# Masks by source tile and an earlier sum of two directions in the head stage of an mLSTM / HGRN2 block

## The reference, cut to what matters

```python
M_HEADS = 8; M_DK = 64; M_DV = 128

def mlstm_scan(q, k, v, ig, lf, state):
    causal = jnp.tril(jnp.ones((L, L), dtype=bool))
    def step(carry, xs):
        ...
        d = jnp.where(causal, b[..., :, None] - b[..., None, :] + ic[..., None, :], -jnp.inf)
        m_t = jnp.maximum(inter, jnp.max(d, axis=-1))
        s = jnp.einsum('bhtd,bhsd->bhts', qc, kc) * jnp.exp(d - m_t[..., None])
        num = jnp.einsum('bhts,bhsv->bhtv', s, vc) + ...
        den = jnp.sum(s, axis=-1) + ...
        h = num / jnp.maximum(jnp.abs(den), jnp.exp(-m_t))[..., None]
    ...

def bidirectional_scan(scan_fn, ctx_fwd, ctx_bwd, lat_fwd, lat_bwd, state0):
    hc_f, st_f = scan_fn(*ctx_fwd, state0)
    hc_b, st_b = scan_fn(*[_flip_t(a) for a in ctx_bwd], state0)
    hl_f, _ = scan_fn(*lat_fwd, st_f)
    hl_b, _ = scan_fn(*[_flip_t(a) for a in lat_bwd], st_b)
    return hc_f + _flip_t(hc_b), hl_f + _flip_t(hl_b)
```

## Time and profile before

| | us |
|---|---|
| median of 3 runs | 1911.44 (1909.27 to 1913.52) |
| the profiled execution's own time | 1908.46 |
| its span | 1906.7 |
| head stage, in the span | 206.0 to 294.7 |
| PE busy in the span | 1787.2 (94%) |
| POOL busy in the span | 132.1 (7%) |

### The profile page before, as it was taken

One profiled execution on the slowest core, in us unless ns is written; L12 is line 12 of the kernel. 1 busy time (PEld: TensorE's weight loads), 2 busy tenths in 40 slices (PEclk: granted clock), 3 DMA queues, 4 the chain that ended last, 5 costly groups with the idle time before them and its releaser, 6 DMA issues. The chain is left out here.

```text
span 1906.7 us, 23789 instructions
## 1 busy us (share of the span) xinstructions
PE 1787.2 (94%) x8836; PEld 1475.6 (77%) x8836; DVE 1372.7 (72%) x1457; ACT 1032.7 (54%) x1249; POOL 132.1 (7%) x138
## 2 busy tenths in 40 slices
PE   7999887899999998899997869999999999999997
PEld 2688676787887876788886758888888888888886
DVE  3676378755554555677449558898989898989898
ACT  2543454522122125422344447888888787878775
POOL 2251120000000000100003020000000000000002
PEclk9999898899999999899998969999999999999999
DMA  7544253444433552344220339999999999999996
GB/s 270 177 144 144 67 188 101 159 144 150 159 133 112 180 184 99 111 166 155 100 77 1 148 117 342 347 407 356 401 355 404 354 402 355 404 350 405 354 407 223
DMA packets 148809, 436.23 MB, mean 229 GB/s; under 512 B 8395, under 2 KB 31091, under 8 KB 148606
## 3 DMA queue, kind: packets, MB, share of 16 engines
q1 hardware_dynamic: 146232, 430.92, 61.5%
q0 software_dynamic: 1152, 4.19, 0.6%
q10 hardware_dynamic: 1350, 0.11, 0.1%
HBM read 416.59 MB, written 16.25 MB: 227 GB/s over the span
## 5 line engine op out<-in xcount | busy, mean ns | idle before, releaser
L2910 DVE TENSOR_TENSOR w_low<-e_ring,w_high 128x1536 fp32r<-128x1536 f32 x383 | 611.6, 1621 | 84.7 <-ACT w_high L2814 83.9
L2814 ACT ACTIVATE w_high<-e_ring 128x1536 fp32r<-128x1536 f32 (+1 forms) x381 | 520.1, 1380 | 157.9 <-PE ps L2732 126.0
L2730 PE MATMUL ps<-w_high,list_h 128*128 128x512 f32 (+1 forms) x768 | 290.6, 378 | 4.2 <-DVE list_l L2928 4.2
L2732 PE MATMUL ps<-w_high,list_l 128*128 128x512 f32 (+1 forms) x768 | 286.8, 373 | 0.0
L2731 PE MATMUL ps<-w_low,list_h 128*128 128x512 f32 (+1 forms) x768 | 286.7, 373 | 0.0
L1791 ACT ACTIVATE fw_high<-ring 128x1024 fp32r<-128x1024 f32 x62 | 65.7, 1060 | 263.2 <-PE ps L1720 191.2
L1842 DVE TENSOR_TENSOR fw_low<-ring,fw_high 128x1024 fp32r<-128x1024 f32 x62 | 76.0, 1225 | 149.8 <-ACT fw_high L1791 149.7
L2730 PEld LDWEIGHTS ps<-w_high,list_h 128*128 128x128 f32 x768 | 144.8, 188 | 25.9 <-issue 4.6
L2732 PEld LDWEIGHTS ps<-w_high,list_l 128*128 128x128 f32 x768 | 144.6, 188 | 21.2
L2731 PEld LDWEIGHTS ps<-w_low,list_h 128*128 128x128 f32 x768 | 144.9, 189 | 20.7
L1718 PE MATMUL ps<-u_high,fw_high 128*128 128x512 f32 x352 | 141.0, 400 | 7.8 <-DVE fw_low L1842 7.8
(11 more groups left out here) (450 smaller groups left out, 3349.6 us busy)
## 6 DMA issues: line engine op xcount, KB each, us to landing
e_ring<-in_e_w_gu_dram SPq DMA_DIRECT2D x96, 1536.0 KB, 9.1
e_ring<-in_e_w_down_dram SPq DMA_DIRECT2D x48, 1536.0 KB, 8.7
bg_area<-in_mod_w_dram SPq DMA_DIRECT2D x72, 512.0 KB, 4.2
e_ring<-in_e_w_gu_dram SPq DMA_DIRECT2D x32, 1024.0 KB, 7.9
ring<-in_f_w_gu_dram SPq DMA_DIRECT2D x22, 1024.0 KB, 7.8
ring<-in_h_w_in_dram SPq DMA_DIRECT2D x10, 2048.0 KB, 8.4
e_ring<-in_e_w_down_dram SPq DMA_DIRECT2D x16, 1024.0 KB, 7.1
ring<-in_m_w_in_dram SPq DMA_DIRECT2D x6, 2048.0 KB, 8.3
```

The lines of the kernel that those rows point to most:

```text
L2730: nc.tensor.matmul(out, high[:, f, :], w_high[:, c, :], start=(f == 0), stop=False)
L2732: last = nc.tensor.matmul(out, low[:, f, :], w_high[:, c, :], start=False, stop=(f == total - 1))
L2814: nc.scalar.activation(piece(k.w_high, p), raw_piece(k, p), ACT.Copy).then_inc(S.high_done, 1)
L2910: nc.vector.tensor_tensor(piece(k.w_low, p), raw_piece(k, p), piece(k.w_high, p).bitcast(F32), ALU.subtract).then_inc(S.low_done, 1)
```

## The change

POOL's mask is cut in four: one instruction for each source tile, each behind that tile's own weighing, where one instruction for all four stood behind the last weighing. PE's one wait for the mask of a turn becomes a wait for each target tile, for the mask of the last source tile it has. And POOL adds a head's two directions in the even turn that follows them, where it was in the odd one after that.

```diff
             def values(n):
                 h, d = n // 2, n % 2
-                pe.wait_ge(masked, n + 1)
                 if n >= 2:
                     pe.wait_ge(summed, n - 1)
                 for i in (0, 1, 2, 3) if d == 0 else (1, 2, 3, 0):
                     js = SOURCES[d][i]
+                    pe.wait_ge(masked, 4 * n + max(js) + 1)
                     if n and i == (3 if d == 0 else 0):
                         pe.wait_ge(summed, n)
...
             for n in range(turns):
                 d = n % 2
-                pool.wait_ge(probs, 4 * n + 4)
-
-                flat = k.u_area[:, d * NT * T:(d + 1) * NT * T]
-                diag = bass.AP(flat.tensor, flat.offset, [list(flat.ap[0]), [T + P, NT], [1, P]])
                 sign = 1 if d == 0 else -1
-                pool.affine_select(out=diag, in_=diag, compare_op=ALU.is_ge, fill=0.0, base=0,
-                                   pattern=[[0, NT], [sign, P]], channel_multiplier=-sign).then_inc(masked, 1)
-                if d == 1 and n > 1:
+                for j in range(NT):
+                    pool.wait_ge(probs, 4 * n + j + 1)
+                    diag = prob[:, d, j, j * P:(j + 1) * P]
+                    pool.affine_select(out=diag, in_=diag, compare_op=ALU.is_ge, fill=0.0, base=0,
+                                       pattern=[[sign, P]], channel_multiplier=-sign).then_inc(masked, 1)
+                if d == 0 and n:
                     add(n // 2 - 1)
             add(HEADS - 1)
```

## The result

Over 20 executions each the changed kernel took 1917.14 us (1910.89 to 1920.94), the kernel before 1909.57 (1900.30 to 1921.39); ratio 1.0037, 95% interval 1.0023 to 1.0051. The forecast was 1912.7 in a range of 1907.5 to 1916.0, most likely within 0.2%. It was wrong: the time lies 1.1 us above the range, and the change costs some 7 us instead of 1.3. The profiled execution took 1913.7 us with a span of 1911.9, so the profile shows a milder case than the median.

A forecast was written before the change was run, and what follows sets the result against it. The head stage, a chain from one head's scores to the next, was taken as the only place of gain or loss; +0.3 at head 2, becoming about 0.5, then +1.0 -0.4 +1.0 -0.4 -0.4 made +1.3: 1912.7 us, range 1907.5 to 1916.0.

The forecast's parts named there:

- Turn 0, masks by tile: Turn 0 of the head stage: value sums start sooner behind per-tile masks, leaving -0.7 us at the end of head 1's scores.
- Masks elsewhere, waits on PE: Other turns: sooner masks are off the path and worth nothing; 48 more PE waits were also taken as nothing.
- What the earlier sum frees: Heads 3 and 5: without L1334's wait for POOL each takes 8.31 us, -0.4 us each, -0.8 together.
- What it runs into: Turns 2, 4 and 8: POOL's sum meets two DVE subtractions, costing 1.03 us each, +3.1 us on the path.
- Rival A: Turns 2, 4 and 8: VectorE keeps its ports through both subtractions, so no cost; 1908.8 us, chance 0.15.
- The end of the stage: Turn 15, last of the head stage: the finish starts sooner because POOL's sum came earlier, -0.4 us.
- The sum: Whole head stage: the gains and losses on the path add up to +1.3 us, median 1912.7 us.
- Rival B: Before head 5's scores: longer PE idle time makes TensorE's clock fall a third time; +4.3 us, 1915.7 us, chance 0.12.
- the meeting of turn 8: Turn 8: POOL's sum overlaps two DVE subtractions, adding 1.0 us on the path before head 5's scores.
- Rival C: Turn 0: TensorE's clock comes back sooner because PE works 0.9 us earlier; 1909.4 us, chance 0.12.
- The range: Whole kernel: 1907.5 us (A and C together, with spread) to 1916.0 us (B); within 0.2% given 0.80.

The follow-up runs named there:

- e10: Changed kernel with the sum where it stood before and waits by target tile in turn 0 only, one wait elsewhere: 1917.1 us, ratio 1.0058.
- r3: e10 run again unchanged: 1915.7 us, ratio 1.0040 to the kernel before.
- e5: Changed kernel with the sum where it stood before and one PE wait for all four masks in every turn: 1911.5 us, ratio 1.0016.
- e8: Kernel before with only the sum one turn sooner, made to wait for DVE's subtraction pairs so they don't overlap: 1907.7 us, ratio 1.0003.
- e2: Changed kernel with the sum put back where it stood before, masks and waits by tile kept: 1915.1 us, ratio 1.0028.
- r1: Kernel before, unchanged, run again against itself: 1907.2 us, ratio 0.9979.
- e12: Changed kernel, unchanged, run again: 1917.1 us, ratio 1.0060 to the kernel before.
- e1: Kernel before with only the sum one turn sooner, one mask and one wait kept: 1918.0 us, ratio 1.0043.
- e3: Changed kernel with POOL's sums of heads 0, 1 and 3 waiting for DVE's subtraction pairs, so they don't overlap: 1915.6 us, ratio 1.0023.
- e7: Changed kernel with the sum waits of e3 and the repeated products of e4: 1907.8 us, ratio 0.9996.
- e4: Changed kernel with the value sums of turns 2, 4 and 8 done twice to fill PE's idle time: 1909.6 us, ratio 1.0007.

## Why the prediction was wrong, point by point

- *Turn 0, masks by tile.* Right in size: the scores of head 1 start 1.26 us sooner (1.3 forecast) and end 0.66 sooner (0.7). Wrong in taking that for a gain: with four masks and this edit alone among PE's waits the kernel is 0.4 to 0.6% slower (e10, r3), where with four masks and one wait it is 0.16% (e5), and what they lack is clock.
- *Masks elsewhere, waits on PE.* The 0.29 us a mask is right; the value sums of two turns in a row take 5.11 us with three more waits in each, where those of one turn took 2.50 before. No cost of their own.
- *What the earlier sum frees.* Right: 8.31 us for heads 3 and 5 forecast, 8.33 and 8.32 in e8. In the changed kernel itself both are covered by the clock (11.47 and 9.64 us).
- *What it runs into.* Right in place and price: +0.96 us in each of turns 2, 4 and 8, 1.03 forecast, and the other three pairs at 1.39. Rival A is refuted; POOL got in between the two subtractions in all three turns. That fits the rule of the Trainium skill (SBUF — State Buffer, "Who interferes with whom") that the one issued first holds the ports and the other is blocked: the sum waited for the first subtraction, the second one for the sum. The cost is 0.96 us, not the sum's full 1.28.
- *The end of the stage.* -0.54, 0.4 forecast.
- *The sum.* Its path terms came to +1.3, of which 0.2 by the slow stretch of head 2; the same terms measure +0.8 (the +0.2 of the table with the 0.6 of head 1's scores). **The step that failed is the one that let TensorE's clock stand as the one trace before showed it**: two stretches, with the same effect on both kernels. Rival B had the mechanism, its price for one fall (3.0; head 3 lost 3.17) and its total of 1915.7, but as a single further fall with a chance of 0.12, and with the meeting of turn 8 as its only cause. The clock is lower in the changed kernel by 0.003 over 20 executions, some 4.5 us by the fitted slope; heads 3 and 5 both fall in both of its profiles, beside a shorter fall at head 2 and a new one behind turn 0, and they fell as well behind 1.94 us of idle time with no meeting (e2). Beside it stood the premise that a gain or loss comes from the head stage or nowhere; outside it one kernel's two profiles differ by 4.1 us.
- *Rival C*, the clock coming back sooner in turn 0, is refuted: it stayed low for 6.8 us (6.9 before), and the earlier start went with less clock, not more.
- *The range.* It was built on three executions between 1909 and 1914. Over 130 executions the kernel before spreads from 1899 to 1922; its spread was itself a sign that the clock, which it follows, decides more here than any term of the sum.

What stays open: what makes the clock fall. The same idle times stand ahead of falls in some executions and ahead of none in others (2.00 us at head 3 in r1 and in the first profile), and earlier value sums in turn 0 go with a lower clock without a reason that a trace shows. Nor does the fit agree with the stage: the changed kernel is 3.4 us (e12: 2.3) slower at equal clock, where the profiles' sum has 0.2 to 0.8, so that of the 7.9 us between the means some 4.5 are the clock's by the fit and the rest is unexplained. At equal clock the meetings look dearer (3.9 us between e8 and e1, 5.1 between e3 and the changed kernel, 1.6 between e7 and e4) than the 2.9 us of the pairs. That they differ so much among themselves says that the fit doesn't hold to better than 2 us, as said above; I take the pairs' 2.9 as the price.

## What to carry to other kernels

Where TensorE waits for other engines in a loop of a few microseconds, count its idle time as carefully as the path: an edit that shortens its work or lets it start sooner can leave the path as it is and lengthen the piece in which it idles, and each fall of the clock behind such a piece cost 1.3 to 3.2 us here, though not every such piece had one behind it. Before work is moved to an engine "that has time", look at what VectorE does at that moment: a subtraction of two SBUF arrays and a GpSimd sum didn't run side by side here, while a multiplication that reads PSUM did. And where single executions of a kernel differ by 1%, one profile shows one pattern of the clock; take its path terms from it, but the clock's share from many executions.

## What the runs showed of the hardware

- Two VectorE subtractions of 64x512 with both inputs in SBUF took 2.35 us for 1.39 when a GpSimd sum of 128x512 became ready during the first: the sum ran between the two, three times out of three in each of the four profiles that have the meeting. It took 1.63 us for 1.28. The weighing (PSUM and one SBUF input) beside the same sum kept its 1.82 us.
- Four GpSimd masks of 128x128 took 0.29 us each (1.04 for four in a row), where one strided one over the same elements took 0.64.
- 60 redundant PE instructions of 129 columns in three idle places took the mean clock of the whole execution from 0.958 to 0.960 and the ratio from 1.0037 to 1.0007; in the kernel before, the same 60 changed neither (0.9607 for 0.9611, ratio 1.0001). The changed kernel's stage became 5.9 us shorter, the cost of the three falls that went.
- The clock fell at head 3 behind 2.00 us of idle time in one profile of the kernel before and not in the other, and outside the head stage the same code took 1812 to 1823 us in seventeen profiles.
- Time followed the mean granted clock by 1.59 us for 0.001 over 330 executions of the kernels in the table, with 1.1 us of scatter left.
